# Eight gather slots instead of six, and two of each eight V rows summed on VectorE

## The reference, cut to what matters

```
act = gelu(einsum('td,tkd->tk', h, u_tab[idx])) * gate      # k = 128 picks a token
out = einsum('tk,tkd->td', act, v_tab[idx])
```

## Time and profile before

| | us |
|---|---|
| median of 3 runs | 4728.89 (4700.46 to 4732.91) |
| profiled execution, span | 4716.4 |
| PE, DVE, POOL, ACT busy | 3914.0, 2652.1, 2057.6, 1793.2 |
| PE L1347, the picks | 2553.0 |
| DVE L947, the picks | 1546.1 |
| DMA engines, mean over the span | 310 GB/s |

### The profile page before, as it was taken

How to read it: one execution, slowest core, us unless ns; L and a number is a source line. 1 busy time by engine, 2 the same in 40 slices (tenths; PEclk the granted TensorE clock), 3 DMA queues, 4 the chain that set the end, 5 groups by cost and what they waited for, 6 DMA issues and landing times.

```text
span 4716.4 us, 45285 instructions
## 1 busy us (share of the span) xinstructions
PE 3914.0 (83%) x8916; PEld 1686.1 (36%) x8916; DVE 2652.1 (56%) x5680; ACT 1793.2 (38%) x4613; POOL 2057.6 (44%) x2765
## 2 busy tenths in 40 slices
PE   8999889778779788878878978977887887887777
PEld 4554444333334333323323323333332332333222
DVE  2339922554745744854764674584475466457444
ACT  3443230243343344344344334334434433433444
POOL 0002230344454555455454544545545445544665
PEclk9999999889899899989998988989998999999999
DMA  2014461789899899899988999999989899989998
GB/s 104 27 37 159 161 255 62 284 339 378 325 356 362 343 354 354 339 354 354 357 346 336 354 351 350 350 350 358 353 337 374 337 347 357 355 332 354 389 407 361
DMA packets 210634, 1462.42 MB, mean 310 GB/s; under 512 B 25616, under 2 KB 25744, under 8 KB 41872
## 3 DMA queue, kind: packets, MB, share of 16 engines
q0 software_dynamic: 194880, 1377.92, 75.5%
q1 hardware_dynamic: 15568, 82.43, 4.9%
HBM read 1424.61 MB, written 35.65 MB: 310 GB/s over the span
## 4 chain that ended last, share of the span: by engine, by line
PE 28%; DMA 19%; DVE 16%; issue 12%; POOL 9%; ACT 5%; DVEq 2%; POOLq 1%; ACTq 1%
DMA arena<-in_uv,st 19%; PE ps L1347 16%; PE ps L1377 7%; POOL arena L493 5%; DVE arena L947 4%; DVE arena L899 4%; POOL st L491 3%; PE ps L1333 3%; ACT arena L669 1%; PE ps L1371 1%; ACT gated L667 1%; DVE CI L1000 1%; DVE arena L1003 1%; ACTq L666 1%; DVE CI L1009 1%
## 5 line engine op out<-in xcount | busy, mean ns | idle before, releaser
L1347 PE MATMUL ps<-arena 128*128 128x512 f32 x5120 | 2553.0, 649 | 679.0 <-ACT arena L669 678.3
L947 DVE SCALAR_TENSOR_TENSOR arena<-arena 128x1024 f32<-128x1024 f32 x1280 | 1546.1, 1224 | 1363.2 <-DMA arena<-in_uv,st 1361.7
L493 POOL DMA_INDIRECT arena<-in_uv,st x1280 | 1434.5, 1121 | 1066.9 <-POOL st L491 805.6
L1347 PEld LDWEIGHTS ps<-arena 128*128 128x128 f32 x5120 | 1014.8, 206 | 2189.2 <-ACT arena L669 1122.8
L665 ACT ACTIVATE acts<-dots 128x1 f32<-128x1 f32 x1280 | 258.4, 202 | 2039.7 <-DVE arena L947 1999.7
L491 POOL COPY st<-arena 128x1 uint32 (+1 forms) x1280 | 491.1, 384 | 837.1 <-PE ps L1347 813.1
L1377 PE MATMUL ps<-arena 128*128 128x512 f32 x1280 | 562.0, 592 | 0.0
L669 ACT ACTIVATE arena<-ident,gated 128x128 f32<-128x128 f32 x1280 | 514.0, 402 | 90.8 <-issue 3.7
L1377 PEld LDWEIGHTS ps<-arena 128*128 128x128 f32 x1280 | 243.1, 190 | 305.7 <-issue 305.7
L1231 PE MATMUL ps<-arena 128*128 128x512 f32 (+1 forms) x768 | 279.5, 524 | 3.5 <-DVE arena L787 2.9
L667 ACT ACTIVATE gated<-arena,acts 128x1 f32 (+1 forms) x640 | 188.5, 295 | 74.0 <-issue 5.0
(11 more groups left out here) (184 smaller groups left out, 1997.7 us busy)
## 6 DMA issues: line engine op xcount, KB each, us to landing
arena<-in_items SPq DMA_DIRECT2D x32, 1024.0 KB, 5.4
arena<-in_uv,st POOLq DMA_INDIRECT x1280, 7.8
qk_scratch<-arena POOLq DMA_DIRECT2D x32, 256.0 KB, 2.7
wp_scratch<-arena POOLq DMA_DIRECT2D x32, 256.0 KB, 6.0
vo_scratch<-arena POOLq DMA_DIRECT2D x32, 256.0 KB, 2.5
arena<-qk_scratch SPq DMA_DIRECT2D x2, 4096.0 KB, 14.0
arena<-vo_scratch SPq DMA_DIRECT2D x2, 4096.0 KB, 21.3
arena<-wp_scratch SPq DMA_DIRECT2D x2, 4096.0 KB, 27.3
```

The source lines that it names most:

```text
L493: g.indirect_dma_start(out=ring[r], out_offset=None, in_=a["uv"], in_offset=bass.IndirectOffsetOnAxis(ap=st[:, r:r + 1], axis=0))\
L947: v.scalar_tensor_tensor(out=ring[r][:, 0:D], in0=ring[r][:, 0:D], scalar=1.0, in1=H[par], op0=ALU.mult, op1=ALU.mult, accum_out=dots[:, r ...
L1347: ins = t.matmul(ACC[par][:, half * BANK:(half + 1) * BANK], diag[:, r * P:(r + 1) * P], ring[r][:, D + half * BANK:D + (half + 1) * BANK] ...
```

## The change

The ring gets eight slots (128 / 8 = 16 turns, no tail). Slots 1 and 5 (BY_DVE) no longer go to PE: ACT stops after `gated`, and VectorE, two picks later (LAG), adds gated x V into a tile ACCV in SBUF. PE works the other six, and at the end of a block adds ACCV to the accumulator with an identity matrix (`merge`). POOL issues straight from the column of IDXC; `st` and its copy go, the four quarter copies stay. `diag` lies in the U half of the slot. The tables count picks instead of turns; in FIRST and SECOND every place is six times the old one, in STEADY the places are new. Room in SBUF comes from smaller work tiles of the choice and from `dynamic_dma_scratch_size=2048`.

```diff
-R = 6
+R = 8
...
+BY_DVE = (1, 5)
...
+LAG = 2
...
-STEADY = dict(norm=3, sc=(4, 5), soft=6, xo=(7.5, 8.5), x2=9.5, tr=10.5, q=(11.5, 12.5, 13.5, 14.5),
-              top=(12.5, 14.5, 16.5, 18.5), cand=(13, 15, 17, 19), expert=(13.5, 15.5, 17.5, 19.5))
+STEADY = dict(norm=18, sc=(22, 27), soft=32, xo=(38, 43), x2=48, tr=53, q=(58, 68, 80, 92),
+              top=(64, 78, 92, 106), cand=(69, 83, 97, 111), expert=(73, 87, 101, 115))
...
+            def gather(b, k):
+
+                r = k % R
+                if r in BY_DVE:
+                    hold(row_summed, b * DVE_PICKS + dve_rank(k) + 1)
+                else:
+                    hold(row_used, b * PE_PICKS + pe_rank(k) + 1)
                 g.indirect_dma_start(out=ring[r], out_offset=None, in_=a["uv"],
-                                     in_offset=bass.IndirectOffsetOnAxis(ap=st[:, r:r + 1], axis=0))\
+                                     in_offset=bass.IndirectOffsetOnAxis(ap=IDXC[:, k:k + 1], axis=0))\
                  .then_inc(row_load[r], 16)
...
-                act.activation(gated[:, r:r + 1], GAT[par][:, ds(k, 1)], ACT.Copy, scale=acts[:, r:r + 1])
+                ins = act.activation(gated[:, r:r + 1], GAT[par][:, ds(k, 1)], ACT.Copy, scale=acts[:, r:r + 1])
+                if r in BY_DVE:
+                    ins.then_inc(gated_ready, 1)
+                    return
                 act.drain()
-                act.activation(diag[:, r * P:(r + 1) * P], ident[:, :], ACT.Copy, scale=gated[:, r:r + 1])\
+                act.activation(diag[r], ident[:, :], ACT.Copy, scale=gated[:, r:r + 1])\
                    .then_inc(diag_ready, 1)
...
             def final(b, par):
 
-                act.wait_ge(row_used, (b + 1) * PICKS + R)
+                act.wait_ge(merged, b + 1)
...
                  .then_inc(dot_ready, 1)
...
+                s = r - LAG
+                if s not in BY_DVE:
+                    return
+                rank = BY_DVE.index(s)
+                rows = ring[s][:, D:2 * D]
+                hold(gated_ready, b * DVE_PICKS + group * len(BY_DVE) + (rank + 1))
+                if type(group) is int and group == 0 and rank == 0:
+                    if type(b) is not int or b >= 1:
+                        hold(merged, b)
+                    ins = v.tensor_scalar(ACCV, rows, gated[:, s:s + 1], None, ALU.mult)
+                else:
+                    ins = v.scalar_tensor_tensor(ACCV, rows, gated[:, s:s + 1], ACCV, ALU.mult, ALU.add)
+                ins.then_inc(row_summed, 1)
...
+            def merge(b, par):
+
+                t.wait_ge(row_summed, (b + 1) * DVE_PICKS + len(BY_DVE))
+                for half in range(2):
+                    ins = t.matmul(ACC[par][:, half * BANK:(half + 1) * BANK], ident[:, :],
+                                   ACCV[:, half * BANK:(half + 1) * BANK], start=False, stop=True)
+                ins.then_inc(merged, 1)
...
-    nc = bacc.Bacc("TRN2", target_bir_lowering=False, num_devices=1)
+    nc = bacc.Bacc("TRN2", target_bir_lowering=False, num_devices=1, dynamic_dma_scratch_size=2048)
```

More of the change, by code:

```diff
@@ L90, with pe_rank, dve_rank @@
         JOBS += [("gate", w, int(_kind == "a"), _c) for w in "ax"]
-R = 6
+R = 8
 GROUPS = PICKS // R
-TAIL = (2, 3)
-assert GROUPS * R + len(TAIL) == PICKS
-USES = [GROUPS + (r in TAIL) for r in range(R)]
-STEADY = dict(norm=3, sc=(4, 5), soft=6, xo=(7.5, 8.5), x2=9.5, tr=10.5, q=(11.5, 12.5, 13.5, 14.5),
-              top=(12.5, 14.5, 16.5, 18.5), cand=(13, 15, 17, 19), expert=(13.5, 15.5, 17.5, 19.5))
[L108 to L116, removed]
+BY_DVE = (1, 5)
+BY_PE = tuple(r for r in range(R) if r not in BY_DVE)
+LAG = 2
+assert GROUPS * R == PICKS
+def pe_rank(k):
+    return k // R * len(BY_PE) + BY_PE.index(k % R)
+def dve_rank(k):
+    return k // R * len(BY_DVE) + BY_DVE.index(k % R)
+PE_PICKS, DVE_PICKS = GROUPS * len(BY_PE), GROUPS * len(BY_DVE)
+STEADY = dict(norm=18, sc=(22, 27), soft=32, xo=(38, 43), x2=48, tr=53, q=(58, 68, 80, 92),
+              top=(64, 78, 92, 106), cand=(69, 83, 97, 111), expert=(73, 87, 101, 115))
+FIRST = dict(norm=18, sc=(24, 30), soft=36, xo=(42, 48), x2=54, tr=60, q=(66, 3, 9, 15),
+             top=(72, 9, 18, 27), cand=(75, 12, 21, 30), expert=(78, 15, 24, 33))
+MIX_TURN = {1: 0, 2: 18, 3: 30, 4: 36, 5: 48, 6: 54, 7: 72, 8: 75, 9: 78}
+MIX_TURN_VECTOR = {**MIX_TURN, 3: 36, 5: 54}
+SECOND = dict(norm=39, sc=(45, 51), soft=57, xo=(63, 69), x2=75, tr=81,
+              q=(84, 90, 96, 102), top=(90, 99, 108, 117), cand=(93, 102, 111, 120),
+              expert=(96, 105, 114, 123))
 Q = 4
 QP = PICKS // Q
-QUARTER_TURNS = [QP * (q + 1) // R for q in range(Q)]
+ARENA = 51444 + 2 * 2 * D + PICKS
 def taker(job):
@@ L224, in build @@
         iota = sb("iota", TOPK)
-        st = sb("st", R, u32)
         dots, acts, gated = sb("dots", R), sb("acts", R), sb("gated", R)
-        ring = [GR[:, r * 2 * D:(r + 1) * 2 * D] for r in range(R)]
+        ring = [GR[:, r * 2 * D:(r + 1) * 2 * D] for r in range(R - 2)]
+        ring += [GR2[:, r * 2 * D:(r + 1) * 2 * D] for r in range(2)]
+        diag = [rows[:, 0:P] for rows in ring]
         qk = QK.rearrange("p (k n) -> p k n", k=KD)
@@ L230, in build @@
         wp = [w.rearrange("p (k n) -> p k n", k=KD) for w in (WPA, WPB)]
-        SV, SIF = XC[:, 0:256], XC[:, 256:512]
-        CV, I0, I1, E0 = (XC[:, 512 + i * 128:640 + i * 128] for i in range(4))
+        SV, SIF, SI = XC[:, 0:64], XC[:, 64:128], XC[:, 128:192].bitcast(u32)
+        CI16 = XC[:, 192:224].bitcast(u32)
+        I0, I1, E0 = (XC[:, 224 + i * 32:256 + i * 32] for i in range(3))
         HI = E0.bitcast(u32)
+        CV = XC[:, 384:512]
         CAND = AC[:, 2 * TOPK * TOPK:]
@@ L300, in build @@
             ("t3_done", "h_ready", "s_done", "ex_in", "ex_out"))
-        idx_ready, idx_taken, st_ready = (sem(n) for n in ("idx_ready", "idx_taken", "st_ready"))
+        idx_ready, idx_taken = (sem(n) for n in ("idx_ready", "idx_taken"))
         row_load = [sem(f"row_load{r}") for r in range(R)]
         dot_ready, diag_ready, row_used = (sem(n) for n in ("dot_ready", "diag_ready", "row_used"))
+        gated_ready, row_summed, accv_ready, merged = (sem(n) for n in
+            ("gated_ready", "row_summed", "accv_ready", "merged"))
         pool_held, sp_held, dve_held = sem("pool_held"), sem("sp_held"), sem("dve_held")
@@ L502, in _ @@
                     hold(idx_taken, Q * b + (q + 1))
[L503 to L510, removed]
+                    for k in range(q * QP, (q + 1) * QP):
+                        gather(b, k)
         @block.scalar
@@ L679, in walk @@
                             for r in range(R):
-                                k = i * R + (at + r)
-                                pick(b * PICKS + k, par, k, r)
+                                pick(b, par, i * R + (at + r), r)
                         at += whole * R
                     else:
-                        pick(b * PICKS + at, par, at, at % R)
+                        pick(b, par, at, at % R)
                         at += 1
[L687 to L690, removed]
             def final(b, par):
-                act.wait_ge(row_used, (b + 1) * PICKS + R)
+                act.wait_ge(merged, b + 1)
                 act.activation(PF[1], ACC[par], ACT.Square, accum_out=fms)
@@ L746, in _ @@
             choose(1, upto, SECOND, 0, Q)
-            upto(GROUPS)
-            tail(0, 0)
+            upto(PICKS)
             with act.Fori(0, (NB - 2) // 2) as pair:
@@ L756, in _ @@
                     choose(b + 1, upto, STEADY, 0, Q)
-                    upto(GROUPS)
-                    tail(b, par)
-            walk(NB - 1, 1, 0, 1)
+                    upto(PICKS)
+            walk(NB - 1, 1, 0, 6)
             final(NB - 2, 0)
-            walk(NB - 1, 1, 1, GROUPS)
-            tail(NB - 1, 1)
+            walk(NB - 1, 1, 6, PICKS)
             final(NB - 1, 1)
@@ L949, in pick, with walk @@
                  .then_inc(dot_ready, 1)
-            def walk(b, par, lo, hi):
-                at, end = int(lo * R), int(hi * R)
+                s = r - LAG
[11 more added lines that the diff above has]
+                ins.then_inc(row_summed, 1)
+            def walk(b, par, at, end):
                 while at < end:
-                    whole = (end - at) // R if at % R == 0 else 0
+                    whole = (end - at) // R if at % R == 0 and at else 0
                     if whole:
@@ L963, in walk @@
                         at += 1
-            def tail(b, par):
-                for r in TAIL:
-                    pick(b, par, GROUPS, r)
             def top16(q):
                 src = bank(4 + q)
-                sets = [(4 * q + j, src[:, j * NK:(j + 1) * NK], AC[:, j * NK:(j + 1) * NK]) for j in range(4)]
+                sets = [(j, src[:, j * NK:(j + 1) * NK], AC[:, j * NK:(j + 1) * NK]) for j in range(4)]
                 for m, s, _ in sets:
@@ L988, in cand_top @@
                 v.drain()
[L989 to L990 removed]
```

(39 more changed lines are left out.)

95 lines of the change are left out of this document (43 added, 52 removed).

## The result

The changed kernel takes 4323.75 us, median of four runs (4319.44 to 4330.06), against 4723.93 for the kernel before; the ratio is 0.9163, with an interval of 0.9135 to 0.919. The forecast was 4330 in a range of 4140 to 4580.

The account below looks back on a forecast made before the run. A six-slot ring going round too slowly, with POOL at 2.48 us a pick, holds middle blocks 66 us over the DMA floor. 4716.4 - 372 (middle) - 30 (block 0) + 3 (last) = 4317, plus 12.5 to the median: 4330, range 4140 to 4580.

Parts of the forecast that it names:

- The floor: Least time of a middle block by DMA transfers: 128 picks at 2.48 us, 320 us with x and y.
- the cushion: Delay that the DMA does not feel thanks to two more slots: 2 x 2.48 = 5.0 us.
- POOL's own chain: POOL's issue, copy and 0.81 us wait at each pick: 2.48 us, so it cannot make up a late slot.
- TensorE's relief: PE takes 96 picks a block instead of 128: 255 us, regaining 1.19 us a pick with a backlog.
- The choice: Choice of experts, picks 64 to 115: DVE needs 143.2 us, DMA 126.5; 11.7 us lost a middle block.
- The first half: Picks 0 to 64 of a middle block: standstills at `norm`, `soft`, `x2` with `tr` lose 8 us (0 to 25).
- (a): Rival: the ring hides everything and the DMA never stops; blocks of 320 to 328, 4184 us; 15 in 100.
- (b): Rival: chains of attention and choice are not hidden; blocks of about 360, 4500 us; 18 in 100.
- (c): Rival: memory gives only 350 GB/s while other engines use SBUF; 4700 us; 4 in 100.
- (d): Rival: DVE stands at its sums, waiting behind ACT 32 times a block; 4940 us at 4 us each; 4 in 100.
- (e): Rival: skipped picks idle PE, its clock dips towards 1.2 GHz; over 5200 us if fully; 2 in 100.
- (f): Rival: the pace stays, as an unpriced wait takes the ring's place; about 4720 us; 2 in 100.

Follow-up runs that it names:

- the spread: Changed kernel with LAG = 1 and the choice's steps over picks 60 to 118, 16 a quarter instead of 14: 4289.26 us (LAG = 1 without that: 4301.23).

## Why the prediction was right, point by point

**What bounds it.** Right, but for POOL. The floor was taken from the last block, 2.48 us a pick, and the middle blocks came to within 21 us of 320. The cause, a ring that goes round too slowly beside other work, is shown by the runs with all picks on TensorE: 382.1 us a block with six slots, 346.4 with eight, and nothing else changed. The slots are a cushion, as the prediction had it, and do not speed up a ring that is slow everywhere: in the quiet last block the same run with six slots keeps the full rate.

```profile
4560.00:4580.00 20.00, 15.97 (x34) 5.42 (x32) 9.87 (x16) 7.30 (x25) 13.40 (x8) 1.00 1.01 422
```

The prediction put the cushion at 5.0 us and took it off twice, in the choice and at `norm`; the 35.7 us that the slots brought are seven times 5.0. At how many standstills of a block they pay was not counted.

What was wrong is that POOL, at 2.48 us a pick, cannot make up for a late slot. It read POOL's own chain from a stretch where the DMA sets the pace and an issue takes 1.37 us. With slots free, an issue takes 0.96 us and the kernel before issues 2121.72 - 2119.75 = 1.97 us apart, copy and wait included:

```profile
2119.75 0.96 POOL L493 DMA_INDIRECT arena<-in_uv,st  x1 [0.81 <-PE ps L1347]
...
2121.72 0.96 POOL L493 DMA_INDIRECT arena<-in_uv,st  x1 [0.81 <-POOL st L491]
```

So it won back 0.5 us a pick even with the copy, which fits the copy's small price of 7.1 and 9.5 us a block.

**The parts.** From before to after the middle block goes 386.5, 379.4 (copy gone), 382.1 (new places and code, still six slots, all on PE), 346.4 (eight slots), 341.0 (sums on DVE). So in this order the slots carry four fifths; the sums bring 5.4 us with eight slots and cost 3.6 with six. The prediction did not price the parts apart, and it let TensorE's relief look like a large part of the cure, since PE regains only 0.76 us a pick; that step was over-weighted. With eight slots and all picks PE works 303 of 346 us, and giving a quarter of the picks away brings no more than the 5.4 net. The relief was also smaller than forecast: 255 us a block expected for PE, 266 measured; the granted clock was 0.89, against 0.95 with all picks on PE.

**POOL.** 1.49 us a pick expected, 1.25 measured where it issues in a burst; 1.97 with the copy.

**VectorE.** The sum was put at 1.22 us, 37 to 42 us a block; it measured 1.28, 40.5 a block with the block's first. The choice, pick 64 to 115, was put at 143.2 us, 11.7 of them lost after the cushion. In one block:

```profile
2454.89:2593.16 138.27, 102.75 (x200) 42.99 (x200) 131.16 (x351) 51.84 (x152) 54.84 (x50) 0.88 0.97 390
```

These are 51 products, 12 sums and all steps of the choice but the first `top`, which ends at 2454.89. Without its 5.28 us the prediction's sum is 137.9 us; DVE took 138.3, busy for 95% of it. At 390 GB/s instead of 422 the DMA engines lost 10.5 us of this stretch, where 11.7 were forecast. Right in size, then, but DVE's excess is not the whole reason. The same picks with all rows on TensorE, where DVE is busy for 88%:

```profile
2460.51:2593.70 133.19, 119.33 (x264) 50.85 (x262) 117.38 (x339) 57.26 (x165) 58.12 (x55) 0.96 1.00 412
```

Without the sums, too, they stand 6.7 us over the DMA's 126.5. And the spread, which takes DVE's excess away on paper, won back only 2.6 us a block. What else holds these picks is not settled.

**The first half.** 8 us; a block of 341.0 less 320 less 10.5 leaves 10.5 for the first half and the end together.

**Block 0 and the last.** 30 less expected, 18 measured. Without the sums block 0 gives 32, so it is the sums, with their merge, that cost more beside the seven quarters of choice than the 1.22 / 4 us a pick they were given; what holds them there was not tried. In the last block 3 more expected, 11.5 less measured, since it, too, has other work beside its first picks, the end of the block before, which I had left out (that this is the cause was not tried). With 364 for 372 in the middle the errors nearly cancel, by luck: 4317 expected for the span, 4322.9 measured. The 12.5 us that I added from span to median did not recur either (1.96 us in the profiled execution, 4324.86 less 4322.9); with 2 in its place the forecast would have been 4319, 5 us under the median instead of 6 over it.

**The rivals.** (a) and (b) bracket the result. (c), memory at 350 GB/s beside busy engines, is out: middle blocks ran at 394 to 401. The Trainium skill, "DMA: Bandwidth & Descriptors", section "Bandwidth", gives about 358 GB/s to each core when both cores of a memory stream; with this core alone the trace shows no such limit, at 394 to 401 in the middle blocks. (d) is out: 5.6 us of waits at the sums. (e): the dips came, and cost nothing where they were foreseen, in the quiet last block:

```profile
4130.00:4150.00 20.00, 14.41 (x26) 5.42 (x25) 12.36 (x19) 6.38 (x22) 9.48 (x9) 0.84 1.01 422
```

The clock is 0.84, the rate 422 GB/s, as at 1.00 before. What the lower clock costs in the middle blocks (0.89 on average, 0.92 before) was not tried. (f), an unpriced wait in the ring's place, is out: a block became 45.5 us shorter.

## What to carry to other kernels

For a ring of slots fed by DMA, compare the quietest stretch with the busy ones of the same kernel. Here six slots held 422 GB/s in the quiet stretch and 355 beside other work: the slots were a short cushion, and two more brought 35.7 us of 382 a block. What a ninth would bring was not tried; the floor is the DMA's own time. An engine that looks too slow inside such a ring may only look so: taking a quarter of the picks from TensorE brought 5.4 us a block, so try the slots before moving work elsewhere. POOL issues in order, so a slot that comes back late holds up the free ones behind it, as in the rows of POOL above.

## What the runs showed of the hardware that was not expected

The first sum of a block, a `tensor_scalar` of 128x1024 without accumulation, needs 0.75 us, where the sums with an accumulator as third operand need 1.28 and the product with h 1.22:

```profile
2290.13 0.75 DVE L961 TENSOR_SCALAR arena<-arena,gated 128x1024 f32<-128x1024 f32 x1
```

And a DMA share near 1 does not mean the full rate. These are two windows of a middle block of the changed kernel, with equal shares and 396 against 415 GB/s:

```profile
2380.00:2400.00 20.00, 20.00 (x45) 8.78 (x45) 12.31 (x18) 7.77 (x24) 9.54 (x9) 0.95 1.00 415
2400.00:2420.00 20.00, 19.32 (x45) 8.28 (x44) 12.97 (x19) 11.02 (x27) 9.08 (x9) 1.00 1.00 396
```
